# Moving small tasks between the steps of a pipelined attention stage, and four window copies from ScalarE to VectorE

## The reference, cut to what matters

```
x = x + 0.5 * swiglu(rmsnorm(x), ffn1...)
h = rmsnorm(x) @ w_in                      # 2290 columns
h_a, h_b, h_c = split(h)
o_a = mla_mixer(h_a, ...)                  # 6 latent heads, q and k of 64 + 32 columns
o_b = nsa_mixer(h_b, ...)                  # 6 heads, 2 groups: compressed, selected, windowed
o_c = diff_mixer(h_c, ...)                 # 4 differential heads, two halves of 32 columns
x = x + concat(o_a, o_b, o_c) @ w_out
x = x + 0.5 * swiglu(rmsnorm(x), ffn2...)
```

```
blk = (t[:, :, cmp_idx] + pe).reshape(B, G, n_cmp, CMP_LEN * DH)
k_cmp, v_cmp = silu(blk @ phi_1) @ phi_2
p_cmp = softmax(mask(q @ k_cmp)) * cmp_mask
o = g0 * p_cmp @ v_cmp + g1 * o_slc + g2 * o_win     # g = sigmoid(gate logits)
```

## Time and profile before

| | us |
|---|---|
| median of 3 runs (1684.67 to 1686.69) | 1685.85 |
| the profiled execution, its own time | 1685.85 |
| the profiled execution, span from first to last instruction | 1684.0 |
| TensorE busy | 1623.6 |
| VectorE busy | 1082.8 |
| ScalarE busy | 878.0 |
| GpSimd busy | 76.2 |
| first attention stage of the second block | 880.78 to 935.95 |
| second one | 1404.11 to 1460.24 |

### The profile page before, as it was taken

The page is one execution under the profiler, slowest core; times in us unless marked ns, Lnnn a source line. Parts: engine busy times, 40 slices in busy tenths (PEclk is TensorE's granted clock), DMA queues, the critical chain, the costliest instruction groups (busy, mean ns, idle before and its releaser), DMA issues.

```text
span 1684.0 us, 24296 instructions
## 1 busy us (share of the span) xinstructions
PE 1623.6 (96%) x9570; PEld 1373.5 (82%) x9570; DVE 1082.8 (64%) x1349; ACT 878.0 (52%) x1301; POOL 76.2 (5%) x142
## 2 busy tenths in 40 slices
PE   7999999989999999999998999999999999999997
PEld 7868888986788878888986788888888887688886
DVE  5767656776756576565657565657665665675655
ACT  6556444655544454444647554445444556654443
POOL 1000000010000002000002000002000001000000
PEclk9999999999999999999999999999999999999999
DMA  9325555540555547555440355556655542056551
GB/s 284 127 76 169 181 199 175 175 163 29 181 199 179 199 163 226 193 183 193 142 159 9 101 175 199 174 199 201 205 184 194 168 151 76 2 184 199 185 193 62
DMA packets 202955, 271.68 MB, mean 161 GB/s; under 512 B 4824, under 2 KB 175440, under 8 KB 202880
## 3 DMA queue, kind: packets, MB, share of 16 engines
q1 hardware_dynamic: 200016, 263.39, 47.3%
q0 software_dynamic: 2544, 7.09, 1.8%
q10 hardware_dynamic: 320, 0.18, 0.0%
HBM read 269.58 MB, written 1.05 MB: 161 GB/s over the span
## 4 chain that ended last, share of the span: by engine, by line
PE 90%; DVE 4%; ACT 3%; issue 1%; DMA 1%; POOL 0%; DVEq 0%; SPq 0%; POOLq 0%; ACTq 0%
PE pair L1781 30%; PE pair L1783 15%; PE bank L1714 11%; PE bank L1716 11%; PE bank L1715 11%; PE bank L1929 1%; PE pair L1910 1%; PE bank L1959 1%; ACT probs L820 1%; PE pair L1714 1%; PE pair L1716 1%; PE pair L1715 1%; DMA raw<-in_w_mem_kv 1%; DVE negmax L1168 1%; DVE w_lo L1039 1%
## 5 line engine op out<-in xcount | busy, mean ns | idle before, releaser
L1781 PE MATMUL pair<-xt,w_hi 128*128 128x512 f32 x2112 | 753.1, 400 | 2.5 <-DVE xt L1048 2.2
L1039 DVE TENSOR_TENSOR w_lo<-raw,w_hi 128x2048 fp32r<-128x2048 f32 x248 | 567.4, 2290 | 148.6 <-ACT w_hi L690 147.2
L690 ACT ACTIVATE w_hi<-raw 128x2048 fp32r<-128x2048 f32 x248 | 473.9, 1915 | 272.3 <-PE pair L1783 200.7
L1783 PE MATMUL pair<-xt,w_lo 128*128 128x256 f32 x2112 | 594.3, 281 | 0.0
L1781 PEld LDWEIGHTS pair<-xt,w_hi 128*128 128x128 f32 x2112 | 399.1, 189 | 101.9 <-issue 3.9
L1783 PEld LDWEIGHTS pair<-xt,w_lo 128*128 128x128 f32 x2112 | 401.0, 190 | 2.3
L1714 PE MATMUL bank<-w_hi,hid_hi 128*128 128x512 f32 x528 | 207.3, 393 | 0.0
L1716 PE MATMUL bank<-w_lo,hid_hi 128*128 128x512 f32 x528 | 206.4, 391 | 0.0
L1715 PE MATMUL bank<-w_hi,hid_lo 128*128 128x512 f32 x528 | 205.8, 390 | 0.0
L1088 DVE TENSOR_TENSOR gate_sum<-pair,gate_sum 128x512 f32<-128x512 f32 x66 | 45.7, 692 | 208.0 <-ACT gate_sum L768 208.0
L1714 PE MATMUL bank<-w_hi,xt 128*128 128x256 f32 (+1 forms) x544 | 163.2, 300 | 0.4 <-DVE xt L1048 0.4
(11 more groups left out here) (271 smaller groups left out, 1506.8 us busy)
## 6 DMA issues: line engine op xcount, KB each, us to landing
raw<-in_w_gate_up SPq DMA_DIRECT2D x44, 1024.0 KB, 5.1
raw<-in_ffn_wg SPq DMA_DIRECT2D x44, 1024.0 KB, 5.3
raw<-in_ffn_wu SPq DMA_DIRECT2D x44, 1024.0 KB, 5.4
raw<-in_ffn_wd SPq DMA_DIRECT2D x44, 1024.0 KB, 5.0
raw<-in_w_in SPq DMA_DIRECT2D x30, 1024.0 KB, 5.4
raw<-in_w_down SPq DMA_DIRECT2D x22, 1024.0 KB, 5.0
raw<-in_w_o SPq DMA_DIRECT2D x8, 1024.0 KB, 5.1
raw<-in_w_out SPq DMA_DIRECT2D x8, 1024.0 KB, 5.0
```

The lines of the kernel that those rows point to most:

```text
L690: act.activation(w_hi[s][:, :], raw[s][:, :], ACT.Copy).then_inc(hi_ready, 1)
L1039: dve.tensor_tensor(w_lo[s][:, :], raw[s][:, :], w_hi[s][:, :].bitcast(F32), ALU.subtract)\
L1781: pe.matmul(out[:, 512 * m:512 * (m + 1)], w[0][:, c, cols], xt[:, 2 * SEQ * c:2 * SEQ * (c + 1)], start=(c == 0), stop=False)
L1783: last = pe.matmul(out[:, 512 * m + SEQ:512 * (m + 1)], w[1][:, c, cols], hi_half(xt, c), start=False, stop=(c == KC - 1))
```

## The change

It does four things, in both layers of the second block.

- The window copies of `q 2`, `kc 0`, `kc 1` and `vc 1` are made by VectorE instead of ScalarE; `q 2` is no longer made ahead of the stage but at the end of step 5.
- The transposes of the places `pe_rows` leave `latents()` and become a task `pe` in the mid of step 0, into `QT_B`; VectorE's copy to `pe_t` leaves `latents_out()` and becomes the hook `places_out`. `pe_t` gets another place in memory.
- VectorE's `window_rope` moves from the mid of step 1, and its `gates` from the mid of step 2, to the end of step 0.
- Tasks change their steps. `k 1` goes from the end of 8 to the end of 6; `back 7` from the mid of 11 to the mid of 8; `forth 7` from the mid of 13 to the end of 9; `pc` 0, 1, 2 from the mids of 9, 10, 12 to the ends of 8, 10, 12. The hooks of VectorE and ScalarE that belong to them move along, and the low half of chunk 6 from the mid of 8 to the end of 7.

The diff:

```diff
--- before.py
+++ after.py
@@ -188,13 +188,13 @@
         windows[f"latent k {i}"] = Windows(10 + i, [("k96", A_DK * i), ("k96", A_DK * (i + 1))], "scalar",
                                            1.0, A_DK)
     windows |= {"q 01": Windows(16, [("proj", B0), ("proj", B0 + P)], "scalar", s),
-                "q 2": Windows(18, [("proj", B0 + 2 * P)], "scalar", s),
+                "q 2": Windows(18, [("proj", B0 + 2 * P)], "vector", s),
                 "ks": Windows(19, [("proj", B_KS - HD), ("proj", B_KS)], "scalar"),
                 "kw": Windows(21, [("proj", B_KW - HD), ("proj", B_KW)], "scalar"),
                 "k 1": Windows(23, [("proj", B_KS + HD), ("proj", B_KW + HD)], "scalar"),
-                "kc 0": Windows(28, [("proj", B_KC - HD), ("proj", B_KC)], "scalar"),
-                "kc 1": Windows(30, [("proj", B_KC + HD), ("proj", B_VC)], "scalar"),
-                "vc 1": Windows(32, [("proj", B_VC + HD)], "scalar")}
+                "kc 0": Windows(28, [("proj", B_KC - HD), ("proj", B_KC)], "vector"),
+                "kc 1": Windows(30, [("proj", B_KC + HD), ("proj", B_VC)], "vector"),
+                "vc 1": Windows(32, [("proj", B_VC + HD)], "vector")}
     pairs = []
     for i in range(C_H // 2):
         for j in range(2):
@@ -210,19 +210,18 @@
                          ("proj", v + HD * ((2 * i + e) // 3))) for e in range(2))
             pairs.append(Pair(a, b, CAUSAL, 3 + i, False, j == 1, ("gate", i, 1 + j)))
     w = "windows"
-    tasks = {0: {"end": [(w, "kc 0")]},
+    tasks = {0: {"mid": [("pe",)], "end": [(w, "kc 0")]},
              1: {"mid": [(w, "kc 1")], "end": [(w, "vc 1")]},
              2: {"mid": [(w, "latent q 4")], "end": [(w, "latent k 4")]},
              3: {"mid": [(w, "q 01")], "end": [(w, "ks")]},
              4: {"mid": [("cmp1",)], "end": [(w, "kw")]},
-             5: {"mid": [("back", 6)]},
-             6: {"mid": [("cmp2",)]},
+             5: {"mid": [("back", 6)], "end": [(w, "q 2")]},
+             6: {"mid": [("cmp2",)], "end": [(w, "k 1")]},
              7: {"mid": [("scores",)], "end": [("forth", 6)]},
-             8: {"end": [(w, "k 1")]},
-             9: {"mid": [("pc", 0)]},
-             10: {"mid": [("pc", 1)]}, 11: {"mid": [("back", 7)]}, 12: {"mid": [("pc", 2)]},
-             13: {"mid": [("forth", 7)]}}
-    return Part(pairs, windows, ["diff q", "diff k", "latent q 0", "latent k 0", "latent q 2", "latent k 2", "q 2"],
+             8: {"mid": [("back", 7)], "end": [("pc", 0)]},
+             9: {"end": [("forth", 7)]},
+             10: {"end": [("pc", 1)]}, 12: {"end": [("pc", 2)]}}
+    return Part(pairs, windows, ["diff q", "diff k", "latent q 0", "latent k 0", "latent q 2", "latent k 2"],
                 tasks, ORDER2)
 
 
@@ -270,7 +269,6 @@
         sink = sb("sink", N_Q)
         sinkt, less_sink = sb("sinkt", 2 * N_Q), sb("less_sink", N_Q)
         lam = sb("lam", 16)
-        angle_at = room[0]
         angle = sb("angle", 56 * 2)
         cos2, sin2 = sb("cos2", 56), sb("sin2", 56)
         posi, posf = sb("posi", NT, I32), sb("posf", NT)
@@ -305,7 +303,7 @@
         q96, k96 = sb("q96", NT * A_H * A_DK), sb("k96", NT * A_H * A_DK)
         uq, ukv = sb("uq", 2 * 576), sb("ukv", 768, at=junk_at - 4096)
         k_cmp, v_cmp = sb("k_cmp", B_H * N_CMP), sb("v_cmp", B_G * HD)
-        pe_t = sb("pe_t", 2 * 16, at=angle_at)
+        pe_t = sb("pe_t", 2 * 16, at=m_base + 1248)
         hid_c, hid_e = (sb(n, 30, at=m_base + 1376 + 256 * i) for i, n in enumerate(("hid_c", "hid_e")))
 
         lat_t = sb("lat_t", 6 * P, at=f_base + 23 * 1024)
@@ -597,9 +595,9 @@
                 .then_inc(tables_landed, 16)
             def blocks(l, w):
 
-                pool.wait_ge(heads_out_a.sem, heads_out_a.at((l, True, ("kc 1", "vc 1")[w])))
+                pool.wait_ge(heads_out_v.sem, heads_out_v.at((l, True, ("kc 1", "vc 1")[w])))
                 if w == 0:
-                    pool.wait_ge(prep_ready.sem, prep_ready.at(("pe_t", l)))
+                    pool.wait_ge(task_out_v.sem, task_out_v.at((l, "pe")))
                     pool.wait_ge(prep_ready.sem, prep_ready.at(("heads", l, "kw")))
                 b4 = blk[w][:, :].rearrange("p (o g n) -> p g n o", o=16, g=B_G)
                 for q in range(2):
@@ -973,8 +971,6 @@
                 def latent_windows(k):
                     copy_windows(SECOND, l, f"latent q {k}")
                     copy_windows(SECOND, l, f"latent k {k}")
-                    if k == 2:
-                        copy_windows(SECOND, l, "q 2")
 
                 def diff_windows():
                     latent_keys()
@@ -1014,7 +1010,7 @@
                 u += 9
                 attend(SECOND, l, {(4, "mid"): [hidden_exp], (5, "mid"): [lambda: back_out(6)],
                                    (7, "end"): [compressed_exp, lambda: forth_out(6)],
-                                   (11, "mid"): [lambda: back_out(7)], (13, "mid"): [lambda: forth_out(7)]})
+                                   (8, "mid"): [lambda: back_out(7)], (9, "end"): [lambda: forth_out(7)]})
                 out_projection(u)
                 u += 4
                 turn_hi(("ffn2", l), 11 + 3 * l, used=u)
@@ -1482,7 +1478,6 @@
                 def latents_out():
 
                     dve.wait_ge(small_mm.sem, small_mm.at(("latent", l)))
-                    link(dve.tensor_copy(pe_t[:, :], bank[3][:, 256:288]), prep_ready, ("pe_t", l))
                     link(dve.tensor_copy(lat_t[:, 0:256], bank[2][:, 0:256]))
                     link(dve.tensor_copy(lat_t[0:HD, 256:512], bank[2][0:HD, 256:512]))
                     link(dve.tensor_copy(lat_t[:, 512:768], bank[3][:, 0:256]), prep_ready, ("lat_t", l))
@@ -1556,6 +1551,11 @@
                 def window_rope():
                     rope(proj[:, :, B_KW:B_KW + 128], 2, HD, 16, 8, ("heads", l, "kw"))
 
+                def places_out():
+
+                    dve.wait_ge(small_mm.sem, small_mm.at(("pe", l)))
+                    link(dve.tensor_copy(pe_t[:, :], QT_B[:, 0:32]), task_out_v, (l, "pe"))
+
                 def hidden_guarded():
 
                     dve.wait_ge(small_mm.sem, small_mm.at(("cmp1", l)))
@@ -1630,15 +1630,14 @@
                     link(dve.tensor_copy(pc_t[:, :], QT_B[:, :]), task_out_v, (l, "pc", i))
 
                 sn = s_cmp[:, 0:180].rearrange("p (i c) -> p i c", c=N_CMP)
-                hooks = {(1, "mid"): [window_rope], (2, "mid"): [gates],
+                hooks = {(0, "mid"): [places_out], (0, "end"): [gates, window_rope],
                          (4, "mid"): [hidden_guarded], (4, "end"): [hidden_sigmoid], (5, "end"): [lambda: diff_sums(6)],
                          (6, "mid"): [compressed_out], (6, "end"): [lambda: diff_norm(6)],
-                         (7, "mid"): [compressed_max],
-                         (8, "mid"): [lambda: chunk_lo(("o2", l, 6), 6, QT_B), compressed_scale],
-                         (9, "mid"): [lambda: compressed_probs(0)], (10, "mid"): [lambda: compressed_probs(1)],
-                         (11, "end"): [lambda: diff_sums(7)],
-                         (12, "mid"): [lambda: compressed_probs(2), lambda: diff_norm(7)],
-                         (13, "mid"): [lambda: chunk_lo(("o2", l, 7), 7, QT_B)]}
+                         (7, "mid"): [compressed_max], (7, "end"): [lambda: chunk_lo(("o2", l, 6), 6, QT_B)],
+                         (8, "mid"): [compressed_scale],
+                         (8, "end"): [lambda: diff_sums(7), lambda: compressed_probs(0)],
+                         (9, "mid"): [lambda: diff_norm(7)], (9, "end"): [lambda: chunk_lo(("o2", l, 7), 7, QT_B)],
+                         (10, "end"): [lambda: compressed_probs(1)], (12, "end"): [lambda: compressed_probs(2)]}
                 projection(u, 9, prepare)
                 u += 9
                 attend(SECOND, l, hooks)
@@ -2040,10 +2039,6 @@
 
                 def latents():
 
-                    pe.wait_ge(phi_landed, 96 * (l + 1))
-                    for w in range(2):
-                        pe.transpose(bank[3][:, 256 + 16 * w:256 + 16 * (w + 1)],
-                                     pe_rows[0:16, P * w:P * (w + 1)], ident[0:16, 0:16])
                     pe.wait_ge(prep_ready.sem, prep_ready.at(("latent", l)))
                     for t in range(NT):
                         pe.transpose(bank[2][:, P * t:P * (t + 1)], proj[:, t, 0:P], ident)
@@ -2082,14 +2077,19 @@
                     pe.wait_ge(prep_ready.sem, prep_ready.at(("ukv", l, 1, 1)))
                     turn_windows(SECOND, l, f"latent q {k}", [(prep_ready, ("latent heads", l))])
                     turn_windows(SECOND, l, f"latent k {k}")
-                    if k == 2:
-                        turn_windows(SECOND, l, "q 2", [(prep_ready, ("heads", l, "q"))])
 
                 def task_of(task):
                     bank_free(SECOND, l, task)
                     out = QT_B
                     name, which = task[0], task[-1]
-                    if name == "cmp1":
```

(10 more changed lines are left out.)

## The result

| | median us | lowest to highest |
|---|---|---|
| before | 1686.01 | 1684.67 to 1686.69 |
| after | 1702.68 | 1701.18 to 1703.55 |

The ratio is 1.0100, with a 95% interval of 1.0088 to 1.0112: 16.7 us slower. The forecast was 11.7 us slower and a range up to 1702.0. The sign was right; the time lies 0.7 us above the range. The profiled execution of the changed kernel took 1703.24 with a span of 1701.5.

A forecast was written before the change was run, and what follows sets the result against it. TensorE, busy for 96% of the span, was taken as the bound, with some 7 us idle per stage. Terms of -0.45 + 2.8 + 3.5 = +5.85 per stage, together +11.7 on 1685.85, gave 1697.5 us, range 1689.5 to 1702.0.

The forecast's parts named there:

- the clock's term: TensorE falling to its lower clock in a stage: about 1 us possible, not certain, nothing put in the sum.
- the walk: Step-by-step following of the first stage's engine queues, doubled for the second: +5.85 us each, together +11.7; chance 0.50.
- over 2 us: TensorE stall at 887, ahead of `turn_probs(0)`, longer than any in the stage before.
- ahead of the stage: Transposes of `pe_rows` and `q 2` leave TensorE's work before the stage, which starts 0.45 us earlier: -0.45.
- `turn_probs(0)` behind the first scores: Sign in step 0: some 8.5 us against 6.09 before, with 2 us or more idle ahead, put down to VectorE's `scale`.
- front part: Steps 0 to 2: VectorE's added copies, gates and ropes delay `scale`, moving `turn_probs(1)` from 891.11 to 893.9: +2.8 us per stage.
- `scores(8)` against `turn_probs(3)`: Steps 5 to 8: VectorE waits for `q 2`, `k 1` waits for `compressed_out`, so `scores(8)` comes 1.5 us later.
- late part: Steps 5 to 13: waits around the moved tasks shift the first output matmul from 935.95 to about 939.45: +3.5 us per stage.
- Part 2 alone: Rival: only steps 0 to 2 cost, the late half is given back; +4.7 us, 1690.6; chance 0.16.
- part 3 alone: Rival: only steps 5 to 13 cost, VectorE overtakes in steps 0 to 2; +6.1 us, 1692.0; chance 0.08.
- Faster: Rival: ScalarE's relief decides, saving its `turn_probs` waits if `scale(0)` is done by 886.8; 8.4 us faster, 1677.4; chance 0.08.
- The clock falls more: Rival: once or twice more in either stage, some 0.96 us each; +1 to +4, 1698.5 to 1701.5; chance 0.09.

The follow-up runs named there:

- the filled kernel: Changed kernel plus 22 matmuls of no use in TensorE's idle time of steps 0 and 1: 1697.95 us against 1686.40 before, ratio 1.0066.
- the tail alone: Kernel before with only `back 7`, `forth 7` and the `pc` tasks moved: 1690.39 us against 1685.53, ratio 1.0025.
- the late part alone: Kernel before with only the change's new steps 5 to 13: 1692.40 us against 1686.40, ratio 1.0036.
- the front part alone: Kernel before with only the change's new steps 0 to 2 and the moved places' transposes and copy: 1694.94 us against 1686.40, ratio 1.0051.
- the ropes alone: Kernel before with only ropes and gates moved to the end of step 0, copies on ScalarE: 1689.31 us against 1685.53, ratio 1.0020.
- the tail with its `pc` tasks in their old places: Kernel before with `back 7` and `forth 7` moved as in the change, `pc` tasks in the mids of 9, 10, 12: 1687.76 us against 1685.98, ratio 1.0007.

## Why the prediction was off

**The step that failed is the clock's term.** The forecast showed the fall in the second stage of before, priced it at 0.96 us, and wrote "I put nothing of it in the sum"; in the rivals it had +1 to +4, a chance of 0.09. In the changed kernel the clock was low for over 13 us in each stage instead of the 3.5 us of the earlier trace rows, and cost 2.60 and 2.73 us by the filled kernel. The forecast's own signs said so: it was to be wrong "if TensorE spends long stretches at the lower clock", and TensorE's busy time in the first stage was to grow by no more than 0.45, where it grew from 47.91 to 54.45. Two errors made it: the stall ahead of `kc 0`, which the walk itself gave, was not seen as the place of the fall (by 884.83, at the end of the 1.22 us of idle for the places' copy, the clock is at the lower level, ahead of the "over 2 us" that the rival named); and a spell was priced as if each were the one of before, where the spells here last several times as long. The Trainium skill (TensorE: Matmul & The Clock Gate, "HAM oscillation — how this bites in real kernels") was the voice for it: it says that waits between groups of matmuls put the engine back on the lower clock, again and again. Both stages of the changed kernel agree, at 0.50 for over 13 us each. The section's case is waits for transfers that are longer than any wait here, so it does not state that 1.22 us can be enough, which the runs show. They also show that a wait need not bring a fall: the tail alone, with the idle time of before in step 0, has 1.00 in both stages.

**The walk held, to 0.5 us in a stage.** With the clock kept, the changed kernel is +11.55 us, against the forecast's +11.7. That it is so close is in part luck. The forecast walked the first stage, at the full clock, and doubled it; the second stage of before has its own fall, 0.96 us, which the filled kernel does not have in its first steps. Against the kernel before with its idle time filled too (1684.83, on the same chip) it is +13.1, and the walk is 1.4 short by medians, 0.8 by the lengths of the stages. Step by step:

| | forecast | measured |
|---|---|---|
| ahead of the stage | -0.45 | -0.56, between the stages |
| `turn_probs(0)` behind the first scores | 8.5 | 8.98 filled, 9.44 |
| front part | +2.8 | +3.0 in the first stage, clock kept |
| `scores(8)` against `turn_probs(3)` | +1.5 | +1.36 |
| late part | +3.5 | +3.84 (+3.83 alone) |
| clock | 0 | +2.60 and +2.73 |

By the stages it adds up like this. The forecast had +6.3 for each. The first grew by 9.40, 3.10 more: 2.60 are the clock and 0.50 the walk. The second grew by 8.34, 2.04 more: 2.73 are the clock, 0.27 the walk, and 0.96 go off for the fall of before. The late part was under by 0.3, most of it in steps 10 to 13, where it made +0.77 (by the late part alone) against +0.55.

**The rivals.** Part 2 alone and part 3 alone are out: both parts cost, each alone and with nothing given back. "Faster" is out: `scale(0)` is done at 890.3, 3.5 us behind its limit of 886.8. "The clock falls more" was the true case. Its highest figure, 1701.5, is 1.2 us below the measured time; it was built from spells of 0.96 each, where the two here cost 5.33 together.

## What to carry to other kernels

Before a copy moves to an engine with a lower busy share, read where that engine stands in the very steps: VectorE was busy for 64% of the span and had 0.57 us of room ahead of the `scale` that TensorE waited for. A task that another engine has to answer should stand ahead of a piece of TensorE work long enough to cover the answer; `pc` behind `turn_probs` instead of ahead of it made 1.9 us in a stage. When a walk through the steps finds a new idle stretch on TensorE (here 1.22 us, ahead of `kc 0`), price a spell at the lower clock with it, and do not take the length of one seen before as the longest (3.5 us before, over 13 us after). Filling the idle time with matmuls of no use tells what the clock is worth. And before a sum made on one stage is doubled, look whether the other stage of the kernel before is in the same state.

## What the hardware showed that I had not expected

TensorE did not get its clock back at once when it was busy again: from 884.83 to 898.20 it was busy for 12.17 of 13.37 us by the profile, at a granted clock of 0.50, while the filled kernel, busy for 12.41 of 14.00 us over the same steps, had 1.00 throughout. What was changed between the two is the idle time, 1.22 us before the `kc 0` transposes, and 1.20 ahead of `turn_probs(0)`. The same idle time did not always lead to the same spell: the front part alone had mean clocks of 0.94 and 0.89 in its two stages, the ropes alone 0.94 and 0.97, and the kernel before fell in one of its two stages behind the 1.07 to 1.08 us of idle that both have. The tail alone, with the same step 0, fell in neither. A short fall can come in the late part too: the second stages of the filled changed kernel and of the tail with its `pc` tasks in their old places have a mean of 0.97 with 1.00 in their first steps, and the latter is 1.2 us longer than its first stage. What decides between them is left open; no run here was made for it.
